# One decoder layer on one core: new step tables for the attention, weights held behind x tiles, square sums moved, last stores split

## What is computed

```
z = rmsnorm(x) @ w_in          # 2304 columns: q 8x64, k 2x64, v 2x64, B, C, h of 512 each
q, k = rope(rmsnorm(q)), rope(rmsnorm(k))
o_attn = softmax with sinks of q k^T over a window of 128, times v   # samples: over a cache of 128 keys
o_conv = B * conv3(C * h)      # causal, depthwise
x = x + concat(rmsnorm(o_attn), rmsnorm(o_conv)) @ w_o
x = x + relu(rmsnorm(x) @ w_up)^2 @ w_down      # 4096 wide
x = x + sigmoid(rmsnorm(x) @ w_ple_gate) * (p @ w_ple)
```

## Time and profile before

| what | value |
| --- | --- |
| median of 3 runs | 1339.88 us (1337.21 to 1344.34) |
| profiled execution, its own time | 1338.31 us |
| its span | 1336.5 us |
| mean granted TensorE clock | 0.992 |
| TensorE busy | 1291.4 us, 97% |
| VectorE (DVE) busy | 713.9 us, 53% |
| ScalarE (ACT) busy | 410.5 us, 31% |
| GpSimd (POOL) busy | 152.4 us, 11% |
| moved by DMA | 73.10 MB |

### The profile page before, as it was taken

How to read it: one execution, slowest core, us unless ns; L and a number is a source line. 1 busy time by engine, 2 the same in 40 slices (tenths; PEclk the granted TensorE clock), 3 DMA queues, 4 the chain that set the end, 5 groups by cost and what they waited for, 6 DMA issues and landing times.

```text
span 1336.5 us, 21762 instructions
## 1 busy us (share of the span) xinstructions
PE 1291.4 (97%) x8348; PEld 1277.9 (96%) x8348; DVE 713.9 (53%) x1289; ACT 410.5 (31%) x822; POOL 152.4 (11%) x205
## 2 busy tenths in 40 slices
PE   5999999989989999999999999999999999999997
PEld 4999998889989899999999999999999999999997
DVE  5666666675776654454453443443544535686442
ACT  5575464454634411121120110111211202353231
POOL 2313332221222200000000000000000000140000
PEclk9999999999999999999999999999999999999999
DMA  8421011011133213111111111111111111111222
GB/s 216 120 81 36 25 30 35 18 37 49 34 83 78 63 48 89 48 47 47 47 46 40 39 47 47 47 47 47 47 47 47 47 47 32 48 52 37 72 72 49
DMA packets 115405, 73.10 MB, mean 55 GB/s; under 512 B 3402, under 2 KB 113894, under 8 KB 115336
## 3 DMA queue, kind: packets, MB, share of 16 engines
q1 hardware_dynamic: 114744, 70.46, 18.9%
q0 software_dynamic: 592, 1.93, 0.5%
q10 hardware_dynamic: 16, 0.00, 0.0%
HBM read 67.79 MB, written 5.54 MB: 55 GB/s over the span
## 4 chain that ended last, share of the span: by engine, by line
PE 75%; DVE 2%; ACT 1%; issue 0%; POOL 0%; DVEq 0%; ACTq 0%
PE acc L1699 68%; PE aux L1699 5%; PE aux L1714 2%; PE aux L1839 1%; DVE conv_rstd L1444 0%; PE aux L1946 0%; ACT xg_hi L1172 0%; DVE xt L1564 0%; DVE xt L1558 0%; DVE aux L1561 0%; PE aux L1789 0%; PE aux L1856 0%; ACT sq_new L1175 0%; DVE conv L1477 0%; POOL sq_sum L887 0%
## 5 line engine op out<-in xcount | busy, mean ns | idle before, releaser
L1699 PE MATMUL acc<-xg_hi,w_hi 128*128 128x352 f32 x960 | 312.8, 326 | 0.0
L1699 PE MATMUL acc<-xg_lo,w_hi 128*128 128x352 f32 x960 | 308.2, 321 | 0.0
L1699 PE MATMUL acc<-xg_hi,w_lo 128*128 128x352 f32 x960 | 308.1, 321 | 0.0
L1699 PE MATMUL acc<-a_hi,w_hi 128*128 128x352 f32 x768 | 247.7, 323 | 0.0
L1699 PE MATMUL acc<-a_lo,w_hi 128*128 128x352 f32 x768 | 246.2, 321 | 0.0
L1699 PE MATMUL acc<-a_hi,w_lo 128*128 128x352 f32 x768 | 245.9, 320 | 0.0
L1612 DVE TENSOR_TENSOR xt<-acc,xt 128x352 f32<-128x352 f32 x192 | 100.3, 522 | 179.2 <-PE acc L1699 178.1
L907 ACT ACTIVATE w_hi<-w_st 128x1024 fp32r<-128x1024 f32 x98 | 103.0, 1051 | 291.6 <-PE acc L1699 291.6
L1699 PEld LDWEIGHTS acc<-xg_lo,w_hi 128*128 128x128 f32 x960 | 181.0, 189 | 0.4 <-issue 0.2
L1699 PEld LDWEIGHTS acc<-xg_hi,w_hi 128*128 128x128 f32 x960 | 180.6, 188 | 0.4 <-issue 0.2
L1699 PEld LDWEIGHTS acc<-xg_hi,w_lo 128*128 128x128 f32 x960 | 180.3, 188 | 0.0
(11 more groups left out here) (207 smaller groups left out, 1645.7 us busy)
## 6 DMA issues: line engine op xcount, KB each, us to landing
w_st<-in_w_up SPq DMA_DIRECT2D x32, 512.0 KB, 4.1
w_st<-in_w_down SPq DMA_DIRECT2D x32, 512.0 KB, 3.4
w_st<-in_w_in SPq DMA_DIRECT2D x18, 512.0 KB, 3.8
w_st<-in_w_o SPq DMA_DIRECT2D x8, 512.0 KB, 3.9
w_st<-in_w_ple_gate SPq DMA_DIRECT2D x8, 512.0 KB, 4.5
x_nat<-in_x_prompt SPq DMA_DIRECT2D x11, 352.0 KB
x_col<-in_x_prompt SPq DMA_DIRECT2D x8, 484.0 KB
out<-y_col SPq DMA_DIRECT2D x8, 484.0 KB
```

The costliest lines, as they stand in the source:

```text
L1699: ins_ = pe.matmul(out, w[a][cols], x[b][tile_], start=(k == 0 and p == 0), stop=(k == len(terms) - 1 and p == 2))
```

## The change

```diff
--- before.py
+++ after.py
@@ -92,23 +92,23 @@
 SUM_AT = {GATED[1] + 1: 0, GATED[2]: 1}
 SPLIT_AT = {g: [n + 2 for n in LAST_FILL if LAST_FILL[n] == g] for g in range(3 * U_OUT)}
 
-X_NORM_AT = {0: [4, 5], 1: [6, 7], 4: [8], 5: [9, 10, 11]}
-X_SQUARE_AT = {-1: [4, 5], 0: [6, 7], 4: [8, 9, 10], 5: [11]}
-X_TURN_AT = {2: [(1, 0), (1, 1), (1, 2), (1, 3), (1, 4)], 3: [(1, 5)], 4: [(1, 6), (1, 7)], 6: [(2, 0), (2, 1), (2, 2), (2, 3)], 7: [(2, 4), (2, 5), (2, 6), (2, 7)]}
+X_NORM_AT = {0: [4, 5], 1: [6, 7], 4: [8, 9], 5: [10, 11]}
+X_SQUARE_AT = {-1: [4, 5], 0: [6, 7], 4: [8, 9], 5: [10, 11]}
+X_TURN_AT = {2: [(1, 0), (1, 1), (1, 2)], 3: [(1, 3), (1, 4), (1, 5), (1, 6)], 5: [(1, 7)], 6: [(2, 0), (2, 1), (2, 2), (2, 3), (2, 4)], 7: [(2, 5), (2, 6), (2, 7)]}
 AHEAD = 4
-VEC_AT = 7
-CACHE_AT = 10
-STORE_AT = 9
-CLEAR_AT = 18
+VEC_AT = 6
+CACHE_AT = 9
+STORE_AT = 3
+CLEAR_AT = 15
 DVE_SPLITS = 23
 
 
-STARTS = {1: 6.0, 2: 11.0, 0: 14.5, 3: 19.0, 4: 22.5, 5: 28.0, 6: 31.5, 7: 37.0, 8: 40.5}
-PE_STEPS = {'B': -0.1, 'S': 3.0, 'Q': 4.35, 'P': 5.75, 'V': 7.0, 'R': 7.15, 'W': 8.2, 'O': 10.5}
-ACT_STEPS = {'B': -0.2, 'E': 1.25, 'S': 3.1, 'Q': 4.3, 'P': 5.55, 'V': 7.2, 'R': 7.2, 'W': 8.1, 'N': 9.15}
-DVE_STEPS = {'B': 0.25, 'E': 1.2, 'S': 3.35, 'Q': 4.25, 'P': 5.8, 'V': 7.35, 'R': 7.2, 'W': 8.2, 'O': 9.9}
-POOL_STEPS = {'B': -0.05, 'E': 2.4, 'Q': 3.7, 'D': 6.5, 'W': 8.3}
-SAMPLE_LATE = {'N': 0.5, 'O': 1, 'E': 0.0, 'P': -1, 'Q': 0.0, 'S': 0.5, 'W': 0.5, 'R': 1.0, 'V': 0.5}
+STARTS = {1: 6.0, 2: 11.0, 0: 14.5, 3: 19.0, 4: 23.0, 5: 27.0, 6: 31.0, 7: 35.0, 8: 39.0}
+PE_STEPS = {'B': -0.25, 'S': 3.1, 'Q': 4.45, 'P': 5.75, 'V': 7.25, 'R': 7.15, 'W': 8.35, 'O': 10.95}
+ACT_STEPS = {'B': -0.1, 'E': 1.55, 'S': 2.25, 'Q': 4.4, 'P': 5.6, 'V': 7.15, 'R': 7.1, 'W': 8.1, 'N': 9.05}
+DVE_STEPS = {'B': 0.1, 'E': 1.05, 'S': 2.85, 'Q': 4.25, 'P': 5.4, 'V': 7.6, 'R': 7.1, 'W': 8.2, 'O': 10.05}
+POOL_STEPS = {'B': -0.7, 'E': 0.1, 'Q': 3.4, 'D': 4.85, 'W': 7.6}
+SAMPLE_LATE = {'N': 0.5, 'O': 0, 'E': 0.0, 'P': -0.5, 'Q': 0.0, 'S': 0.5, 'W': 0.5, 'R': 1.0, 'V': 0.5}
 
 
 def plan_inproj(steps, cache):
@@ -622,8 +622,11 @@
 
             for t in range(XPC):
                 load_x(t)
-            for n in range(3):
-                load(n)
+            sp.wait_ge(x_landed[1], 16)
+            load(0)
+            sp.wait_ge(x_landed[3], 16)
+            load(1)
+            load(2)
             load_x(4)
             load_x(5)
             load(3)
@@ -724,11 +727,20 @@
                     load_pw(s, n)
                 for s in range(2):
                     store_y(s, bass.ds((2 * i + s) * P, P), 3 * i + (Y_USE[(3 * s + 2) % 2] + (3 * s + 2) // 2 + 1))
-            for s in range(2):
-                store_y(s, slice((KT - 2 + s) * P, (KT - 1 + s) * P),
-                        3 * (KT // 2 - 1) + Y_USE[(3 * s + 2) % 2] + (3 * s + 2) // 2 + 1)
-            for s in range(2):
-                sp.wait_ge(y_stored[s], 48 * (KT // 2))
+            store_y(0, slice((KT - 2) * P, (KT - 1) * P), 3 * (KT // 2 - 1) + Y_USE[0] + 2)
+            n = slice((KT - 1) * P, KT * P)
+            body = y_p[XT - NS:SEQ, :].rearrange("(t q) d -> q t d", q=XT)
+            for c in range(NCH):
+                f = NCH + c
+                sp.wait_ge(aux_free[3 + f % 2], 3 * (KT // 2 - 1) + Y_USE[f % 2] + f // 2 + 1)
+                first = max(XPC * c, 1)
+                sp.dma_start(body[:, first - 1:XPC * (c + 1) - 1, n], y_col[0:XT, 1, first:XPC * (c + 1), :])\
+                    .then_inc(y_stored[1], 16)
+                if c == 0:
+                    sp.dma_start(y_p[0:XT - NS, n], y_col[NS:XT, 1, 0, :]).then_inc(y_stored[1], 16)
+                    sp.dma_start(y_s[:, n], y_col[0:NS, 1, 0, :]).then_inc(y_stored[1], 16)
+            sp.wait_ge(y_stored[0], 48 * (KT // 2))
+            sp.wait_ge(y_stored[1], 48 * (KT // 2 - 1) + 80)
             sp.wait_ge(kv_stored, 64)
             sp.wait_ge(tail_stored, 32)
             sp.wait_ge(cache_stored, 32)
@@ -1946,14 +1958,13 @@
                 pe.matmul(aux[bank][:, 0:CH], ones[:, :], sq_sum[:, chunk(c)], start=True, stop=True)\
                     .then_inc(ones_full, 1)
 
-            for c in range(NCH):
-                ones_product(c, c, N1_USE[c], 3 * CT + 3 * (KT - 1) + c + 1)
-
-
-            def mlp_block(i):
+            def mlp_block(i, first=False):
                 for m in range(BLK):
                     pe.wait_ge(wlo_ready, 8 * i + (W_MLP + m + 1))
                     for c in range(NCH):
+                        if first and m == 0 and c == 1:
+                            for c_ in range(NCH):
+                                ones_product(c_, c_, N1_USE[c_], 3 * CT + 3 * (KT - 1) + c_ + 1)
                         pe.wait_ge(xg_lo_ready, 3 * (KT - 1) + c + 1)
                         pe.wait_ge(acc_free[c], G_BLK * i + (U_MLP + m))
                         fill(c, m % 2, xg_in)
@@ -1968,7 +1979,8 @@
                                  for k in range(BLK)]
                         product(acc[f % 3][:, 0:CH], w_in_, a_in, terms).then_inc(acc_full, 1)
 
-            with pe.Fori(0, NBLK - 1) as i:
+            mlp_block(0, True)
+            with pe.Fori(1, NBLK - 1) as i:
                 mlp_block(i)
 
             pe.wait_ge(p_landed, 48)
```

## The result

| | before | after |
|---|---|---|
| median of the runs on this chip, us | 1338.56 (1337.21 to 1344.34, 4 runs) | 1319.03 (1317.86 to 1320.17, 4 runs) |
| profiled execution's own time, us | 1338.3 | 1318.65 |
| its span, us | 1336.5 | 1316.9 |
| mean granted clock of TensorE | 0.992 | 0.999 |

The ratio on record is 0.9839, with a 95% interval of 0.9823 to 0.9855: faster by 1.6%. The ratios in this document are the record's own estimates and not quotients of medians: here the ratio stands for 21.6 us of 1338.6, while the medians differ by 19.5 us and the profiled spans by 19.6. The forecast was 1317.5 us in a range of 1310 to 1331; the median came 1.5 us above the forecast. One of the 29 executions of the kernel before that stand beside e1 to e4 took 1840.56 us at a granted clock of 0.654, and the ratios leave it out.

A forecast was written before the change was run, and what follows sets the result against it. TensorE, busy 97% of the span, was taken as the bound. Gains of 15.0 + 0.8 + 0.8 + 2.8 + 2.8 = 22.2 us took 1338.3 to 1316; with 1.6 up to the median, 1317.5 us, range 1310 to 1331.

The forecast's parts named there:

- attention: Attention among the input projections: new step tables recover 15.0 of at most 20.2 us of TensorE idle and slow clock.
- x turns: Turns at fills 2, 3 and 6: moving the fifth turn gains 1.3 us, about 0.5 lost at fill 6, net 0.8.
- first weights: Kernel start: holding weight loads behind x tiles 1 and 3 lands tile 3 earlier, gaining 0.8 us.
- square sums: MLP start: sums behind the first up product save 2.8 idle plus 1.7 slow clock, less 1.7 root wait: 2.8 us.
- last rows: Kernel end: storing the last rows per chunk leaves one small store behind the last turn, gaining 2.8 us.
- Rival (a): Attention: DVE's in-order queue is late every period, two or three clock drops stay; gain only 5 to 9 us; chance 0.18.
- (b): Attention: the waits only change name; gain 0 to 3 us, total 1330 to 1336; chance 0.08.
- (c): Attention: slower, as S of tiles 4 to 8 and P wait longer for DVE; 1348 at 4.5 us a tile; chance 0.03.
- so the O to V wait goes: Attention: V follows R behind a fill, with O half a fill plus S and R ahead; old longest wait 1.0 us.
- The walk: Attention: one period traced from the end of fill 30 (tile 5), finding waits of 0.5 and 0.8 us.
- P6: Attention, step P of tile 6: waits some 0.8 us because a weight split falls one fill earlier, ahead of B, W and Q.
- rival (d): Kernel start: DMA ring order makes the held loads give 0; total 1318.3 us; counted within the forecast's chance of 0.62.

The follow-up runs named there:

- e1: The kernel before with the new step tables (constants) alone: median 1325.19 us, ratio 0.9884.
- e4: The kernel before with the last column stored chunk by chunk alone: median 1336.2 us, ratio 0.9972.
- e2: The kernel before with the first weight loads held behind x tiles 1 and 3 alone: median 1341.35 us, ratio 0.9996.
- e6: The kernel after with VectorE's split of weight 16 moved behind E of tile 6: 1314.07 us, ratio 0.9815.
- e12: The kernel after, unchanged, run again on the same chip as e6 and e9: 1319.71 us, ratio to the kernel before 0.9853.
- e5: The kernel after without the hold, first weights loaded as before: 1320.2 us, ratio to the kernel before 0.9833.
- e10: The kernel after with all three first weights held until x tile 3 has landed: 1320.25 us, ratio to the kernel before 0.9842.
- e3: The kernel before with the three ones products (square sums) behind the first up fill alone: median 1339.61 us, ratio 0.9988.
- e9: The kernel after with e6's moved split, the first MLP unit's reciprocals reordered on VectorE and its memsets on POOL: 1311.88 us, ratio 0.9788.

## Why the prediction was right, and where it was not

| step | predicted us | measured us | from |
|---|---|---|---|
| attention | 15.0 | 12.4 | windows of after |
| x turns | 0.8 | 0.8 | waits 1.27, 0.45 |
| first weights | 0.8 | 0.05 in this pair of profiles; 0.9 at x tile 3 on average; 0.5 (-1.5 to 2.4) in time | chunk 1's turns; landings; e2 |
| square sums | 2.8 | 2.8 | 2.84 + 1.7 - 1.75 |
| last rows | 2.8 | 3.0 | end of y_col to end of span |
| sum | 22.2 | 19.0 of a span 19.6 shorter | |

- **The table's main claim held.** o_tok and qkv no longer hold up W and V in each pair, the wait of S for a bank freed by pt_lo is gone, and idle plus clock in the attention fell from 20.2 us (13.4 + 4 x 1.7) to 7.8 (6.1 + 1.7). e1 shows it as the tables' doing: the same waits to the tenth, and a span 13.3 us shorter, for the 15.8 that the prediction gave to the tables with the x turns. (The ratio of e1 says 15.6, with 12.7 to 18.5, and can't tell the two.) One sign of being right failed, under 5 us of idle: it was 6.1. Rival (a) would have left 11 to 15 us of that, (b) 17 and more; both fell, and (c) with them. The totals that the prediction writes for (a) and (b), up to 1333 and 1336, don't follow from their gains: 5 to 9 and 0 to 3 us in place of 15.0 give 1323.5 to 1327.5 and 1329.5 to 1332.5. With its own numbers half of (b) stands inside the stated range.
- **The step that failed is "so the O to V wait goes".** It goes in every tile but one. The walk did find the split of weight 16 ahead of E of tile 6, and gave S of tile 6 a wait of 0.5 from it; it was 1.26. It did not follow the delay further down VectorE's queue: pt_lo, the taps and O's copy stand behind E, and O's copy frees the bank that V needs. That is the 1.80 (the sign "no wait of o_tok or qkv by L1839" held only because the profile names another releaser), and with the 1.26 it is half of the 6.1 us of idle; the allowance for what the walk missed was 1.3. e6, with one instruction moved, takes the S wait away and 1.3 of V's, and idle falls from 6.1 to 3.5 us, the figure that the prediction had left. So the attention fell 2.6 us short of its 15.0 by this one backlog.
- **P6** was to wait 0.8 behind the other split; the waits for prob in tile 6 came to 0.23 + 0.33, and 0.82 + 0.33 fell to tile 3, which the walk had under "0.9 around tiles 0 and 3".
- **The count of drops, one, was right in the profile of after** and partly luck: the same kernel showed two in e12, neither at the same place. The two other profiles on the kernel after with its attention unchanged and nothing else but the loads moved (e5, e10) show two as well.
- **The hold: size right, place wrong.** Tile 3 came 0.9 us forward on average, near the 0.8 predicted, though the gain fell at tile 1 and not between tiles 1 and 3, where the prediction looked for it. That "each us that tile 3 lands earlier moves the start of TensorE by one" held, to a few hundredths at the first fill. The forecast's own execution had 0.3 of it, and the time can't tell 0.8 from rival (d), a gain of 0; its reason, ring order, is not what the landings show. With the hold x tile 4 was issued 1.2 us later (12.13 and 10.95), a little over the "at most 1", and that was covered as the prediction said.
- **Square sums and store: right in mechanism and size, by the waits.** The root came late by what the queue of the earlier trace rows said, 1.75 for 1.7. Of the 2.8 for the sums, 1.7 is the clock drop, which e1 was also without while it kept the wait; e3's time says 1.6 (-0.3 to 3.5) and can't decide. The last issue took 0.31, under the 0.9 that the prediction set as its most. From the issue at 1313.97 to the end it is 2.9 us, of which the issue is 0.31 and SP's wait for the landing 2.0, for a store of 180 KB. The fixed cost of about 2.0 us of the Trainium skill ("DMA: Bandwidth & Descriptors", Anatomy of one DMA) is of the same order; the section gives it for DMAs that GpSimd issues, and this one is SP's. The estimate by that page, a gain of 3.1, and the 2.8 worked out from rows lie on both sides of the 3.0, too close to tell apart.
- **The number was nearer than the sum, by luck.** The sum was 2.6 us of span too large (22.2 for 19.6): 2.6 at the attention and most of 0.8 at the start, less 0.2 at the store and 0.6 in small waits that no term had. The median came only 1.5 us above the forecast, because the forecast added 1.6 for the distance from the profiled execution to the median, which after was 0.4.

What stays open: what decides in one execution which of the places has its clock drop, and so how much of a gain under 4 us a single profile can show; and what the hold is worth in time, which the runs give only within 2 us.

## What to carry to other kernels

When a step is moved in a hand-made order over in-order queues, follow its delay to the end of the queue and not only to the next consumer: a split that waits for another engine's backlog held back an add, a copy and a bank, and cost two waits and not one. On an engine that is 54% busy, an idle stretch costs nothing by itself, but what stands behind it in the queue may be what TensorE waits for. And when a wait is removed, price the next consumer of the same result first; here the root, at 1.75 of 4.5 us, was foreseeable to a tenth from the durations before.

## What the runs showed of the hardware

- The same kernel with the same waits, to 0.05 us, had its granted clock drop at 235 us in one execution and at 150 and 372 in another; e6 had none, and e3, whose attention is that of before, had a drop at 36 us and six more up to 333, where before had four between 181 and 330. A drop costs 1.7 us as a rule (4 x 0.18 + 4 x 0.24 above), but those near 36 in e3 and 150 in e9 lasted twice as long: in e9 two windows of 4 us at 0.66 and 0.50.

```profile
148.00:152.00 4.00, 4.00 (x21) 3.68 (x21) 0.97 (x5) 1.84 (x5) 0.00 (x0) 0.66 0.00 0
152.00:156.00 4.00, 4.00 (x18) 3.93 (x17) 0.00 (x0) 0.45 (x1) 0.00 (x0) 0.50 0.02 4
```

- The rise from 1.2 to 2.4 GHz at the start fell between 19.4 and 23.0 us over the kernels, and did not follow the first turn: 12.87 with a rise at 19.4 (e2), 12.15 with one at 22.1 (e10). By the turns of chunk 1, at 32 to 34 us, this left little trace: they stood 22.0 to 22.4 us behind the square of tile 3 in all profiles but e10.
- Waits between engines of the attention repeat to 0.05 us between two profiles of one kernel; landings of the first loads vary by 1 to 2 us at the same issue times (tile 3 at 9.8 to 11.1 with one and the same hold).
- The releaser that a profile names need not be one that the instruction waits for: here, by the code, v_parts of the wrong tile, which ended 0.2 us after O's copy.
- Loads issued behind others slowed them here: x tile 3 came at 11.2 us on average with three weights behind it (five profiles), at 10.3 with one from tile 1 on (eight), at 9.0 with none (one).
